# Five of 32 out-projection parts moved into the chunk recurrence of a mixer layer

## The reference

```
for l in range(2):
    x = x + 0.5 * _swiglu(_rms_norm(x, norm_ffn1[l]), ...)          # FFN1
    proj = _rms_norm(x, norm_mix[l]) @ w_in[l]                      # 1024 -> 2944
    y_rwkv = _rwkv7_mixer(...)      # 6 heads of 64, state recurrence, group norm, gate
    y_attn = _attention_mixer(...)  # 6 heads of 64
    y_conv = _conv_mixer(...)       # 256 channels, 31 taps, layer norm, silu
    x = x + concatenate([y_rwkv, y_attn, y_conv]) @ w_out[l]        # the out-projection
    x = x + 0.5 * _swiglu(_rms_norm(x, norm_ffn2[l]), ...)          # FFN2
```

## Time and profile before

| what | value |
|---|---|
| median of 3 runs | 1394.23 us (1392.06 to 1394.49) |
| the profiled execution, its own time | 1393.89 us |
| its span in the trace | 1391.8 us |
| PE busy | 1355.3 us, 97% of the span |
| DVE, ACT, POOL busy | 71%, 53%, 11% |
| mean granted clock of PE | 0.996 |
| layer 0, recurrence from the first satok product to the first variance | 324.10 to 338.79 us |
| layer 0, from there to the start of FFN2 | 338.79 to 366.48 us |

### The profile page before, as it was taken

The page is one execution under the profiler, slowest core; times in us unless marked ns, Lnnn a source line. Parts: engine busy times, 40 slices in busy tenths (PEclk is TensorE's granted clock), DMA queues, the critical chain, the costliest instruction groups (busy, mean ns, idle before and its releaser), DMA issues.

```text
span 1391.8 us, 24913 instructions
## 1 busy us (share of the span) xinstructions
PE 1355.3 (97%) x9761; PEld 1180.6 (85%) x9761; DVE 994.3 (71%) x1326; ACT 736.0 (53%) x1041; POOL 157.8 (11%) x156
## 2 busy tenths in 40 slices
PE   9999999998999999999999999999999999999996
PEld 7888889977888888888888988788888998788885
DVE  6666666687776666766666776886666675998788
ACT  6444467454754445644446655564444445755552
POOL 3000000196000000000000059200000033000000
PEclk9999999999999999999999999999999999999999
DMA  9866265200775545755529210285662953465621
GB/s 339 262 195 194 96 204 161 77 33 2 245 261 183 196 134 182 262 184 184 178 67 303 77 62 4 91 275 183 192 198 94 304 183 117 152 207 191 200 96 60
DMA packets 172532, 230.57 MB, mean 166 GB/s; under 512 B 4688, under 2 KB 153864, under 8 KB 172198
## 3 DMA queue, kind: packets, MB, share of 16 engines
q1 hardware_dynamic: 169968, 223.75, 49.3%
q10 hardware_dynamic: 1877, 5.59, 1.1%
q0 software_dynamic: 608, 0.12, 0.1%
HBM read 228.39 MB, written 2.63 MB: 166 GB/s over the span
## 4 chain that ended last, share of the span: by engine, by line
PE 87%; DVE 7%; ACT 3%; issue 1%; POOL 1%; POOLq 0%; DVEq 0%; ACTq 0%
PE bank L479 36%; PE bank L639 27%; PE bank L643 14%; PE bank L1447 3%; DVE proj L1927 1%; PE bank L594 1%; PE bank L1320 1%; PE bank L1133 1%; PE bank L1272 1%; PE bank L896 1%; DVE up_lo L464 0%; DVE down_lo L464 0%; DVE gate_lo L464 0%; PE bank L1143 0%; ACT work L1198 0%
## 5 line engine op out<-in xcount | busy, mean ns | idle before, releaser
L464 DVE TENSOR_TENSOR down_lo<-w_down,down_hi 128x2048 fp32r<-128x2048 f32 x67 | 154.9, 2312 | 97.4 <-ACT down_hi L459 97.4
L639 PE MATMUL bank<-hT,up_hi 128*128 128x512 f32 x880 | 220.8, 393 | 0.0
L711 ACT ACTIVATE work<-bank 128x256 f32<-128x256 f32 x176 | 66.8, 384 | 258.6 <-PE bank L643 258.2
L639 PE MATMUL bank<-hT,gate_hi 128*128 128x512 f32 x800 | 199.8, 392 | 0.0
L459 ACT ACTIVATE down_hi<-w_down 128x2048 fp32r<-128x2048 f32 x67 | 128.3, 1915 | 117.6 <-PE bank L479 116.4
L639 PEld LDWEIGHTS bank<-hT,up_hi 128*128 128x128 f32 x880 | 158.2, 189 | 29.2 <-issue 0.6
L464 DVE TENSOR_TENSOR gate_lo<-w_gate,gate_hi 128x2048 fp32r<-128x2048 f32 x66 | 151.6, 2296 | 35.8 <-ACT gate_hi L459 35.6
L464 DVE TENSOR_TENSOR up_lo<-w_up,up_hi 128x2048 fp32r<-128x2048 f32 x72 | 162.5, 2257 | 15.5 <-ACT up_hi L459 15.5
L639 PEld LDWEIGHTS bank<-hT,gate_hi 128*128 128x128 f32 x800 | 147.0, 188 | 28.4
L479 PE MATMUL bank<-down_hi,ff_hi 128*128 128x512 f32 x400 | 156.3, 391 | 0.0
L479 PE MATMUL bank<-down_lo,ff_hi 128*128 128x512 f32 x400 | 156.3, 391 | 0.0
(11 more groups left out here) (366 smaller groups left out, 2301.5 us busy)
## 6 DMA issues: line engine op xcount, KB each, us to landing
w_up<-in_ffn_w_up_dram SPq DMA_DIRECT2D x44, 1024.0 KB, 5.4
w_down<-in_ffn_w_down_dram SPq DMA_DIRECT2D x44, 1024.0 KB, 5.2
w_gate<-in_ffn_w_gate_dram SPq DMA_DIRECT2D x43, 1024.0 KB, 5.4
w_up<-in_w_in_dram SPq DMA_DIRECT2D x12, 1024.0 KB, 9.7
w_down<-in_w_in_dram SPq DMA_DIRECT2D x11, 1024.0 KB, 6.3
w_gate<-in_w_up_dram SPq DMA_DIRECT2D x11, 1024.0 KB, 5.1
w_up<-in_w_up_dram SPq DMA_DIRECT2D x11, 1024.0 KB, 5.1
w_down<-in_w_down_dram SPq DMA_DIRECT2D x11, 1024.0 KB, 5.2
```

The costliest lines, as they stand in the source:

```text
L464: dve.tensor_tensor(staged[kind][1][:, 0:cols], slot[sl][:, 0:cols], staged[kind][0][:, 0:cols].bitcast(F32), ALU.subtract).then_inc(split ...
L639: pe.matmul(bank[:, :], w[0][:, c, at], hpair[:, :, c, :], start=c == 0, stop=False)
L711: act.activation(to[:, q, j * SEQ:(j + 1) * SEQ], psum[2 * q + j][:, SEQ:], ACT.Copy)\
```

## The change

- `OUT_SLOTS` becomes down0, up0, gate0, down1: the second weight tile (k = 1) is staged in `up`, the third (k = 2) in `gate`.
- The four PSUM banks of the out-projection become 2, 3, 6, 7, and variances and spreading go to banks 4 and 5. x is transposed into other banks accordingly (`MIX_PLACES`).
- Chunks 3 to 5 of `mix` are split in two steps instead of one: chunk 4 during the matrix chain before the recurrence, and chunks 3 and 5 behind state 0.
- PE runs five of tile 0's eight parts inside the recurrence: one before and one behind L1521 of the first chunk, two before the third chunk's `st_done` wait, one before the fourth's.
- The second weight tile is split inside the recurrence (ACT and DVE behind chunk 1) instead of behind group norm; taps 2 and 3 move behind state 2.
- The gated y is written into `mix` instead of a buffer of its own, squares and norm rows go into `hT`.
- Behind the recurrence PE's order becomes: 3 parts of tile 0 between variances and spreading, mean, 4 parts of tile 1 (chunk 3), `cl_var`, 4 parts of tile 1 (chunk 2), then tiles 2 and 3.

```diff
-OUT_SLOTS = ["down0", "gate0", "up0", "down1"]
+OUT_SLOTS = ["down0", "up0", "gate0", "down1"]
...
+        MIX_BANKS = (2, 3, 6, 7)
+        MIX_PLACES = [(4, 0), (5, 0), (2, 0), (6, 0), (3, 0), (7, 0), (4, 1), (5, 1)]
...
             for ch in range(4):
...
+                if ch == 2:
+                    pe.wait_ge(S["mix_low"], 2 + past["mix_low"])
+                    out_unit(0, 1, 0, 0)
+                    out_unit(0, 1, 0, 1)
+                if ch == 3:
+                    out_unit(0, 0, 1, 1)
                 if ch > 0:
-                    pe.wait_ge(S["mat_done"], (1 if ch == 1 else 2) + past["mat_done"])
                     pe.wait_ge(S["st_done"], ch + past["st_done"])
...
+                    if ch == 0:
+                        pe.wait_ge(S["mat_done"], 2 + past["mat_done"])
+                        out_ready(0, 1)
+                        out_unit(0, 0, 0, 0)
                     pe.wait_ge(S["sa_done"], ch + 1 + past["sa_done"])
...
+                if ch == 0:
+                    out_unit(0, 0, 0, 1)
...
             variance(0)
-            out_ready(0, 1)
-            out_unit(0, 0)
+            out_unit(0, 0, 1, 0)
             variance(1)
-            out_unit(0, 1)
+            out_unit(0, 1, 1, 1)
             gn_spread(0)
-            out_unit(0, 2)
+            out_unit(0, 1, 1, 0, last=True)
             gn_spread(1)
...
             mm.then_inc(S["cl_mean"], 1)
-            for i in range(3, 7):
-                out_unit(0, i)
+            out_ready(1, 2)
+            for t, h in HALVES:
+                out_unit(1, 1, t, h)
             pe.wait_ge(S["cl_sq"], 1 + past["cl_sq"])
...
             mm.then_inc(S["cl_var"], 1)
-            out_unit(0, 7)
-            out_ready(1, 3)
-            for i in range(8):
-                out_unit(1, i)
-            out_ready(2, 3)
-            for i in range(8):
-                out_unit(2, i)
-            out_ready(3, 4)
+            out_ready(1, 4)
+            for t, h in HALVES:
+                out_unit(1, 0, t, h, last=(t, h) == HALVES[-1])
+            out_ready(2, 4)
+            for j in range(2):
+                for t, h in HALVES:
+                    out_unit(2, j, t, h, last=(j, t, h) == (1, *HALVES[-1]))
+            out_ready(3, 5)
...
         def act_mix(act, uses):
...
+                if i == 18:
+                    act.wait_ge(S["mixa_ready"], 2 + past["mixa_ready"])
+                    act_mixed(act, 4, 5)
...
+                if ch == 0:
+                    act.wait_ge(S["mixa_ready"], 3 + past["mixa_ready"])
+                    act_mixed(act, 3, 6, 2)
                 if ch == 1:
-                    act.wait_ge(S["mixa_ready"], 3 + past["mixa_ready"])
-                    act_mixed(act, 3, 6)
                     act.activation(unused, eps["gn"], ACT.Sqrt)
+                    act_high(act, uses, OUT_SLOTS[1])
...
-            act_high(act, uses, OUT_SLOTS[1])
...
         def dve_mix(dve, uses, link):
...
+                if i == 20:
+                    dve.wait_ge(S["mix_high"], 1 + past["mix_high"])
+                    dve_mixed(dve, 4, 5)
...
                 if ch == 0:
+                    dve.wait_ge(S["mix_high"], 2 + past["mix_high"])
+                    dve_mixed(dve, 3, 6, 2)
...
                     side_tap(0)
                     side_tap(1)
                 if ch == 1:
+                    dve_low(dve, uses, OUT_SLOTS[1])
+                if ch == 2:
                     side_tap(2)
                     side_tap(3).then_inc(S["conv_dve"], 1)
-                if ch == 2:
-                    dve.wait_ge(S["mix_high"], 1 + past["mix_high"])
-                    dve_mixed(dve, 3, 6)
...
-                dve.tensor_tensor(yg[:, k, :].rearrange("p (t c n) -> p t c n", t=NT, c=3),
+                dve.tensor_tensor(parity(mix[:, 0:3, :])[:, k],
...
-            dve_low(dve, uses, OUT_SLOTS[1])
             dve.wait_ge(S["cl_root"], 1 + past["cl_root"])
             link(dve.reciprocal(proj[:, CG + 1, 1:], proj[:, CG, 1:]))
...
             dve_low(dve, uses, OUT_SLOTS[2])
```

More of the change, by code:

```diff
@@ L334, in build @@
         assert o <= o_bh + 3 * 3 * SEQ
-        yg, o = area(o_tok, 2, 384)
-        ysq, o = area(o, 2, 384)
-        gnrows, o = area(o, 2, 384)
+        ysq, gnrows = (spare[:, at:at + 768].rearrange("p (a b) -> p a b", a=2) for at in (0, 2048))
         low, o = area(o_ffn + 3584, 2, 512)
@@ L936, in act_raw @@
             for c in range(4):
-                act_high_part(act, n, RAW_PLACES, c, gain)
+                act_high_part(act, n, places, c, gain)
             act_squares(act, n, COLUMNS, (2,))
             for c in range(4, KC):
-                act_high_part(act, n, RAW_PLACES, c, gain)
+                act_high_part(act, n, places, c, gain)
             act_squares(act, n, COLUMNS, (3,))
         def dve_raw(dve, uses, n, gain, kind, link):
+            places = MIX_PLACES if n == 2 else RAW_PLACES
             dve_residual(dve, uses, kind, n - 1, COLUMNS, range(3), mixed=n > 0)
@@ L948, in dve_raw @@
             for c in range(2):
-                dve_low_part(dve, n, RAW_PLACES, c, gain)
+                dve_low_part(dve, n, places, c, gain)
             dve_residual(dve, uses, kind, n - 1, COLUMNS, (3,), mixed=n > 0)
             for c in range(2, KC):
-                dve_low_part(dve, n, RAW_PLACES, c, gain)
+                dve_low_part(dve, n, places, c, gain)
             dve_rms_rows(dve, n, link)
@@ L1102, in pe_out, with act_mixed, dve_mixed @@
                 mm.then_inc(used[slots[k][:-1]], 1)
-        def act_mixed(act, lo, hi):
-            act.activation(hT[0][:, lo:hi, :], mix[:, lo:hi, :], ACT.Copy).then_inc(S["mix_high"], 1)
-        def dve_mixed(dve, lo, hi):
-            dve.tensor_tensor(hT[1][:, lo:hi, :], mix[:, lo:hi, :], hT[0][:, lo:hi, :].bitcast(F32),
+        def act_mixed(act, lo, hi, step=1):
+            act.activation(hT[0][:, lo:hi:step, :], mix[:, lo:hi:step, :], ACT.Copy).then_inc(S["mix_high"], 1)
+        def dve_mixed(dve, lo, hi, step=1):
+            dve.tensor_tensor(hT[1][:, lo:hi:step, :], mix[:, lo:hi:step, :], hT[0][:, lo:hi:step, :].bitcast(F32),
                               ALU.subtract).then_inc(S["mix_low"], 1)
@@ L1492, in y_of, with out_ready, out_unit @@
                 return mm
+            def out_ready(k, ready):
+                pe.wait_ge(S["mix_low"], ready + past["mix_low"])
+                tile_ready(pe, uses, OUT_SLOTS[k])
+            def out_unit(k, j, t, h, last=False):
+                kind = OUT_SLOTS[k][:-1]
+                w = [t_[:, :].rearrange("p (c n) -> p c n", n=D) for t_ in staged[kind]]
+                c = 2 * OUT_PAIRS[k] + j
+                mm = product(pe, psum[MIX_BANKS[2 * t + h]][:, :], lambda p_: hT[p_][:, c, tokens(t)],
+                             lambda p_: w[p_][:, j, h * 512:(h + 1) * 512], k == 0 and j == 0,
+                             k == 3 and j == 1, skip_group_check=True)
+                if last:
+                    mm.then_inc(used[kind], 1)
+                elif k == 3 and j == 1:
+                    mm.then_inc(S["half_done"], 1)
             for ch in range(4):
@@ L1535, in pe_mix @@
             y_of(3).then_inc(S["y_mm"], 1)
-            def out_ready(k, ready):
-                pe.wait_ge(S["mix_low"], ready + past["mix_low"])
-                tile_ready(pe, uses, OUT_SLOTS[k])
-            def out_unit(k, i):
-                j, t, h = (i // 4, *HALVES[i % 4]) if k < 3 else (i % 2, *COLUMNS[i // 2])
-                kind = OUT_SLOTS[k][:-1]
-                w = [t_[:, :].rearrange("p (c n) -> p c n", n=D) for t_ in staged[kind]]
-                c = 2 * OUT_PAIRS[k] + j
-                mm = product(pe, psum[4 + 2 * t + h][:, :], lambda p_: hT[p_][:, c, tokens(t)],
-                             lambda p_: w[p_][:, j, h * 512:(h + 1) * 512], k == 0 and j == 0,
-                             k == 3 and j == 1, skip_group_check=True)
-                if i == 7:
-                    mm.then_inc(used[kind], 1)
-                elif k == 3 and j == 1:
-                    mm.then_inc(S["half_done"], 1)
             def variance(k):
@@ L1585, in pe_mix @@
             mm.then_inc(S["cl_var"], 1)
-            out_unit(0, 7)
-            out_ready(1, 3)
-            for i in range(8):
-                out_unit(1, i)
-            out_ready(2, 3)
-            for i in range(8):
-                out_unit(2, i)
-            out_ready(3, 4)
-            for i in range(6):
-                out_unit(3, i)
-            pe_turn_first(pe, 2, RAW_PLACES)
-            for i in range(6, 8):
-                out_unit(3, i)
-            pe_turn_next(pe, 2, RAW_PLACES)
+            out_ready(1, 4)
[6 more added lines that the diff above has]
+            out_ready(3, 5)
+            for t, h in COLUMNS[:3]:
+                for j in range(2):
+                    out_unit(3, j, t, h)
+            pe_turn_first(pe, 2, MIX_PLACES)
+            for j in range(2):
```

(5 more changed lines are left out.)

28 lines of the change are left out of this document (15 added, 13 removed).

## The result

The changed kernel takes 1401.28 us (median of 5 runs, 1400.19 to 1401.85) against 1394.49 us before (5 runs, 1392.06 to 1396.91): ratio 1.0046, 95% interval 1.0034 to 1.0057. It is slower by 6.8 us, where 5.8 was forecast. The profiled span went from 1391.8 to 1398.7 us.

A forecast was written before the change was run, and what follows sets the result against it. PE was taken as the bound, busy 97% of the span, so only its idle time could move. Losses of 2.8 and 3.0 us per layer added 5.8 to 1394.23, giving 1400.0 us; range with rival B 1396.0 to 1402.0.

The forecast's parts named there:

- The recurrence ends 2.7 us later: Recurrence, layer 0: its end moves from 338.79 to 341.5, with bounds of 1.9 and 3.5 us.
- step 1: First chunk: the part before L1521 waits for tile 0's low half, making everything later 0.99 us late.
- Step 2: Behind state 0: DVE's new 512-column split takes 1.4 us (lower bound 0.62), so state 1 starts 2.4 late.
- Step 3: Behind state 1: DVE splits the second weight tile; the 0.36 us wait goes, 0.69 of part replaces it; moved taps cost nothing.
- A new wait of 3.0 us, tile 2 1.06 late: Behind cl_var: PE waits for DVE's split of tile 2, queued behind reciprocal and products, and begins it at 355.72.
- FFN2's first tile is next, 1.8 us more: Start of FFN2: late slot and staging pair delay its first split and the residual; PE's transposes start 2.84 us late.
- Sum 2.8 and 3.0 us: Whole kernel: layer 0 loses 2.8 us and layer 1 3.0, together 5.8 us.
- The 0.2 set aside for layer 1's load: Layer 1, FFN2's first tile: 0.2 us more for a load that meets ACT's seven parameter loads.
- rival D: Clock falls in the new wait, tile 2's parts up to 5.6 us longer: up to 1411; chance 0.10 together with E.
- its own signs of being wrong: Wrong if PE does not wait for gate_lo, residuals do not follow FFN2's split at once, or the clock drops.
- Rival C: Behind cl_var: tile 2's split is not late, PE goes on at 352.7, total 1390.3 us; chance 0.08.
- rival B: Start of FFN2: its first split is early enough, only 1.06 us per layer remain, total 1396.4 us; chance 0.15.

The follow-up runs named there:

- e9: e2 with the five parts placed behind cl_var instead of in the recurrence: 1399.16 us, ratio to the kernel before 1.0021.
- e1: Changed kernel with tile 2 of the out-projection split by ACT and DVE ahead of the wait for cl_root: 1392.36 us, ratio to the kernel before 0.9989.
- e4: Changed kernel with only DVE's order changed: two residual steps, FFN2's first gate split, then the third step: 1398.92 us, ratio to the kernel before 1.0038.
- e2: e1 plus DVE's first two residual steps ahead of its split of FFN2's first gate tile: 1389.05 us, ratio to the kernel before 0.9965.
- e10: e9 with matmuls nobody reads before the second and third chunks' waits for the state: 1395.16 us, ratio to the kernel before 1.0004.
- e5: Changed kernel with the five parts taken out of the recurrence and five put behind cl_var: 1404.67 us, ratio to the kernel before 1.0072.
- e6: Changed kernel with DVE's low part of tile 2 computed twice, lengthening PE's wait for gate_lo: 1407.81 us, ratio to the kernel before 1.0090.
- e11: Kernel before, with matmuls nobody reads before the second and third chunks' waits for the state: 1395.21 us, ratio to the kernel before 1.0002.

## Why the prediction was right

By its own steps, for the clean layer 1 and on the count of the table:

- *The recurrence ends 2.7 us later.* 2.2 measured (cl_var 27.39 to 29.60). One term that was off is step 1: the second chunk's L1508 came 0.50 later, not 0.99. It took down_lo's 3.02 us of before as fixed, but that time held a wait for POOL: when the split began, POOL's instruction in flight had 0.87 us to go, in the changed kernel 0.24, and the split took 2.38, so the part ahead of L1521 found it done. Step 2 came to 1.2 us (5.18 to 6.38 from the second to the third chunk) instead of 1.4: the new job took 1.10 us beside POOL, between the bound of 0.62 and the 1.4 taken; without the two parts the wait would have been 2.35 (e9). Step 3's mechanism stood: no wait at the fourth chunk, taps in time. Its size was 0.48 us where the prediction has 0.33, as the part took 0.89 us there and not 0.695.
- *A new wait of 3.0 us, tile 2 1.06 late.* 2.71 measured in both layers; the third tile 0.58 late (35.49 to 36.07), 0.5 less because of step 1. The chain from cl_var to tile 2 was forecast as 6.31 + 0.15 and took 6.47 us (349.18 to 355.65). e1, which takes just the split out of this chain, removes the wait, and the layer is then 0.5 us shorter than before (46.78 against 47.31) with the same longer recurrence.
- *FFN2's first tile is next, 1.8 us more.* 1.79 measured: transposes 2.36 late, of which 0.58 from tile 2. The binding one of the two conditions is the staging pair: ACT's 362.90 was released by PE, while the load (issued at 355.60, 5.5 us to landing) was there at 361.1. In the clean layer 1 it is close: the load landed at 908.3, PE ended tile 2 at 908.6 and ACT began at 908.66. e4 removes this wait by DVE's order alone.
- *Sum 2.8 and 3.0 us.* 2.47 in the clean layer; 3.89 in layer 0. The 0.2 set aside for layer 1's load did not appear. The premise that no product changes and so only idle time can move is not quite so: of the 2.47 us 1.02 are busy time.
- *The clock.* The forecast's sum left it out; rival D came true in one of two layers of the profiled execution, at 1.42 us of its "up to 5.6". This is the step that failed: the sum has the clock at nothing, and the prediction names a drop of the clock among its own signs of being wrong. It more than made up for the recurrence's 0.5 us per layer: 5.8 was forecast, 6.8 measured, 4.9 from the two waits and the recurrence alone (twice 2.47), and 0.4 in the profiled executions lies ahead of the first mixer's last values product. That the sum came within 1 us of the median is in part luck, two errors of opposite sign; the mechanism, two late waits of the lengths forecast, is not.

The range (1396.0 to 1402.0) held the 1401.28. Rival C failed as argued, since DVE runs in order and tile 2's split came behind the whole chain; the prediction's rival B, that only the first wait costs, failed because the profile shows the second wait and e4 what it is worth. Theory B of the experiments, the longer recurrence as the loss, is ruled out by e1.

What the parts' place is worth was never the trouble: with both late waits gone (e2) the change is a gain of 1.7 us per clean layer over the kernel before (45.58 against 47.31), and all of it is the place, since e10, which has e2's orders without it, is back at 47.32. The two parts ahead of the third chunk also fill a wait behind which the clock otherwise falls: it fell behind the unfilled 2.35 us in all three layers that have them (e5's layer 1, both of e9), and in neither layer of e10, where fillers stand there. How much of a median that is stays open. By its places e5 should lie some 2 us above the kernel before, and it lies 9.4 above; e9 should lie level with it, and lies 3.9 above, while its profiled execution lost 6.4 us in stretches that are the same in all kernels.

What stays open is when the clock falls. Of four profiled passes over the unfilled wait of 2.7 us (both layers of the changed kernel, both of e4) it fell behind one; at the 5 us wait of e6 it fell in both layers; in e11 it stood at 0.50 from 340 to 345 us, while PE was busy for 5.00 of 5.00 us; and in the kernel before and the changed kernel it fell near 760 us, in code that no edit touched. No run here gives a condition that holds for all of these, and so the clock's part in the difference of two medians (about 2 us here, an estimate from 6.8 - 4.9) is known only after the fact.

## What to carry to other kernels

Work that is moved to an earlier idle stretch is worth its time only if the next thing in line is already there when PE comes to it: look for what PE will need that much sooner, and where that sits in its engine's queue. A buffer that is used later is also given back later; follow it to the first load and the first split of the next stage. And an engine's order at a stage's border is worth a look of its own: putting two residual steps ahead of a weight split saved 1.2 us per layer here. Last, where the clock moves a median by more than the edit does, compare the same stretch in layers whose granted clock was 1.00.

## What the runs showed of the hardware

- PE's granted clock fell to its lower level (0.50, 1.2 of 2.4 GHz) at many places in these kernels: behind a wait of 2.71 us in one layer and not behind the same wait in the other; behind one of 2.35 us in e5 and e9; in e11 from 340 on, with PE busy for the whole 5 us; in e5 it stayed down for 20 us (875 to 895) over the end of a recurrence of small products and what follows it. The Trainium skill ("TensorE: Matmul & The Clock Gate", section "Why this matters for your kernels") warns of pauses between bursts of matmuls. The falls at the waits of e6 agree with it; e11's fall from 340 on does not follow such a pause, the longest idle time of PE in the 9 us before being 0.36.
- A DVE subtraction of two SBUF tiles took its own time and, to within 0.15 us, what was left of POOL's instruction in flight. The split of 2048 columns, 2.28 us alone, took 3.02 with 0.87 us left of POOL's (kernel before, 321.23), 2.38 with 0.24 left (changed kernel, 321.65) and 2.29 with 0.13 left (332.86); 512 columns, 0.69 alone at 357.63, took 1.10 with 0.56 left. POOL's next instruction was held in turn: about 1 us otherwise, it took 3.00 beside the first of these splits and 2.89 beside each of the other two. Four tap instructions took 2.40 us (336.25, changed kernel) beside a single instruction of POOL's, where they took 3.94 in the middle of its chain (330.65, before).
- Mean granted clock and time go together from execution to execution, though not strictly: e9 1394.0 us at 0.997 and 1404.7 at 0.988, the kernel before 1392.5 at 0.997 and 1404.5 at 0.988, but also 1392.2 at 0.995.
